# Moving the product of weights and values behind the projection, and the division of the weights to that projection, in the attention of the mixer

## The reference

```python
s = jnp.einsum('bqhd,bqjhd->bhqj', qn[:, :, g], kg).astype(jnp.float32) * scale
s = s + biases[g][:, None, :]
m = jnp.max(s, axis=-1, keepdims=True)
e = jnp.exp(s - m)
l = jnp.sum(e, axis=-1, keepdims=True)
o = jnp.einsum('bhqj,bqjhd->bqhd', e / l, vg.astype(jnp.float32))
...
merged = jax.nn.sigmoid(ga) * (ret @ w_ret_o[l]) + jax.nn.sigmoid(gb) * (att @ w_att_o[l])
x = x + gt_a[:, None, :] * (merged @ w_o[l])
```

## Time and profile before

| | us |
|---|---|
| three runs | 2019.44, 2024.46 and 2028.82; median 2024.46 |
| the profiled execution | 2020.84 |
| its span | 2019.0 |
| PE busy | 1853.7, 92% of the span |
| attention with its fillers, from the trace | about 215 to 339 |
| mean granted clock of PE | 0.968 of full |

### The profile page before, as it was taken

One profiled execution on the slowest core, in us unless ns is written; L12 is line 12 of the kernel. 1 busy time (PEld: TensorE's weight loads), 2 busy tenths in 40 slices (PEclk: granted clock), 3 DMA queues, 4 the chain that ended last, 5 costly groups with the idle time before them and its releaser, 6 DMA issues. The chain is left out here.

```text
span 2019.0 us, 25094 instructions
## 1 busy us (share of the span) xinstructions
PE 1853.7 (92%) x10306; PEld 1214.2 (60%) x10306; DVE 754.2 (37%) x1091; ACT 552.2 (27%) x811; POOL 11.7 (1%) x23
## 2 busy tenths in 40 slices
PE   7999998779999999999999999978899997989998
PEld 6799876643333332333333333328789987869996
DVE  5767644431111111111111111106565555655555
ACT  3444554210000000000000000005544434534442
POOL 0000000000000000000000000000000000000000
PEclk9999999779999999999999999989999998989999
DMA  9877642299999999999999999968345546325552
GB/s 332 311 258 237 235 138 74 96 372 429 431 431 432 431 431 432 431 432 431 431 431 431 431 431 431 431 261 285 125 146 177 180 146 208 117 92 167 188 172 100
DMA packets 152474, 592.99 MB, mean 294 GB/s; under 512 B 7603, under 2 KB 82527, under 8 KB 127824
## 3 DMA queue, kind: packets, MB, share of 16 engines
q1 hardware_dynamic: 150176, 583.90, 73.1%
q0 software_dynamic: 2224, 8.04, 1.2%
HBM read 590.84 MB, written 1.07 MB: 293 GB/s over the span
## 5 line engine op out<-in xcount | busy, mean ns | idle before, releaser
L1426 PE MATMUL psum<-expert_ring,expert_arena 128*64 128x512 f32 x2048 | 453.9, 597 | 21.3 <-DMA expert_ring<-in_w_mlp_dram 21.3
L1426 PEld LDWEIGHTS psum<-expert_ring,expert_arena 128*64 128x64 f32 x2048 | 142.2, 137 | 316.8 <-issue 272.6
L320 DVE TENSOR_TENSOR layer_w_lo<-layer_ring,layer_w_hi 128x1024 fp32r<-128x1024 f32 x190 | 231.4, 1224 | 242.3 <-ACT layer_w_hi L315 242.1
L315 ACT CAST layer_w_hi<-layer_ring 128x1024 fp32r<-128x1024 f32 x190 | 197.6, 1047 | 243.6 <-PE psum L365 123.5
L363 PE MATMUL psum<-layer_x_hi,layer_w_hi 128*128 128x256 f32 x864 | 249.9, 289 | 13.2 <-DVE layer_w_lo L320 10.2
L1442 PE MATMUL psum<-expert_ring,expert_arena 128*64 128x512 f32 x1024 | 234.0, 601 | 30.1 <-DMA expert_ring<-in_w_mlp_dram 29.2
L364 PE MATMUL psum<-layer_x_lo,layer_w_hi 128*128 128x256 f32 x864 | 248.7, 288 | 0.0
L365 PE MATMUL psum<-layer_x_hi,layer_w_lo 128*128 128x256 f32 x864 | 248.5, 288 | 0.0
L1314 DVE TENSOR_SCALAR expert_arena<-psum 128x512 f32<-128x512 f32 x32 | 22.1, 692 | 557.0 <-PE psum L1426 557.0
L363 PEld LDWEIGHTS psum<-layer_x_hi,layer_w_hi 128*128 128x128 f32 x864 | 170.4, 197 | 15.6 <-issue 11.8
L1442 PEld LDWEIGHTS psum<-expert_ring,expert_arena 128*64 128x64 f32 x1024 | 68.7, 137 | 176.1 <-issue 117.8
(11 more groups left out here) (271 smaller groups left out, 1983.9 us busy)
## 6 DMA issues: line engine op xcount, KB each, us to landing
expert_ring<-in_w_mlp_dram SPq DMA_DIRECT2D x192, 2048.0 KB, 23.3
layer_ring<-in_w_ffn_in_dram SPq DMA_DIRECT2D x44, 1024.0 KB, 5.0
mixer_ring<-in_w_in_dram SPq DMA_DIRECT2D x38, 1024.0 KB, 6.8
mixer_ring<-in_w_ada_dram SPq DMA_DIRECT2D x24, 1024.0 KB, 5.9
layer_ring<-in_w_ffn_out_dram SPq DMA_DIRECT2D x20, 1024.0 KB, 4.9
layer_ring<-in_b_w_in_dram SPq DMA_DIRECT2D x10, 1024.0 KB, 7.3
layer_ring<-in_w_mix_out_dram SPq DMA_DIRECT2D x8, 1024.0 KB, 5.0
layer_ring<-in_a_w_in_dram SPq DMA_DIRECT2D x7, 1024.0 KB, 9.2
```

Of the source, the lines that this page charges most:

```text
L315: self.nc.scalar.copy(hi, raw).then_inc(self.hi_ready, 1)
L320: self.nc.vector.tensor_tensor(lo, raw, hi.bitcast(FP32), ALU.subtract).then_inc(self.lo_ready, 1)
L1426: last = nc.tensor.matmul(U[CAP * h:CAP * h + CAP, N * n:N * n + N], xg[:, k, j, :], ring[:, at:at + N], start=False, stop=k == KC - 1)
```

## The change

It has two parts. First, `ao{u-1}` is added behind the projection of step u and, for u = 7, behind the eight `mod` jobs. Second, the division of units 0 to 5 hangs at the first job of the projection of step u (`divided_at`); the divisions of units 6 and 7, whose steps have no projection, still hang at `ao5` and `ao6`.

```diff
--- before.py
+++ after.py
@@ -525,6 +525,7 @@
     filler += [(f"{what}{half}", by, w, col + N * half)
               for what, by, w, col in (("ro", "act", A["w_ret_o"][0], 0), ("ga", "act", w_in, 7680), ("gb", "act", w_in, 8704)) for half in range(2)]
 
+    divided_at = {}
     for u in range(len(units) + 1):
         if u:
             for n in range(1 + units[u - 1][1]):
@@ -532,18 +533,17 @@
         if u < len(units):
             jobs.add(f"sa{u}", "act")
             jobs.add(f"sb{u}", "act")
-        if u > 1:
-            jobs.add(f"ao{u - 1}", "dve", high=True)
-        if filler:
-
+        if filler and u < len(units):
+
+            divided_at[filler[0][0] + "t0"] = u
             for _ in range(2 if u == 1 else 1):
                 name, by, w, col = filler.pop(0)
                 jobs.pair(name, by, jobs.rows(w, col))
-            if u == 1:
-                jobs.add("ao0", "dve", high=True)
         elif u == len(units) - 1:
             for n in range(8):
                 jobs.add(f"mod{2 + n // 4}.{n % 4}", "act")
+        if u:
+            jobs.add(f"ao{u - 1}", "dve", high=True)
         some_ada()
     assert not filler and not ada_left
     for half in range(2):
@@ -771,10 +771,12 @@
                     dve.wait_ge(xh_ready, job.hi)
                     dst, src = high_places(job, b, xl)
                     nc.vector.tensor_tensor(dst, src, high_places(job, b)[0].bitcast(FP32), ALU.subtract).then_inc(freed_by_dve, 1)
-                    if name[:2] == "ao" and 1 < int(name[2:]) + 1 < len(units):
+                    if name[:2] == "ao" and int(name[2:]) + 1 < len(units) and int(name[2:]) + 1 not in divided_at.values():
                         divide(int(name[2:]) + 1)
                     continue
                 if job.by != "dve":
+                    if name in divided_at:
+                        divide(divided_at[name])
                     if name[:2] == "ga":
                         half, t = int(name[2]), int(name[4])
                         cols = slice(N * half, N * half + N)
@@ -790,8 +792,6 @@
                         step.mark(nc.vector.tensor_reduce(mx2[:, u % 2, 0:1], ba, AX.XY, ALU.max))
                         step(nc.vector.tensor_reduce(mx2[:, u % 2, 1:2], b[:, 0:w], AX.X, ALU.max))
                         nc.vector.tensor_reduce(negmax[:, u % 2:u % 2 + 1], mx2[:, u % 2, :], AX.X, ALU.max, negate=True).then_inc(max_ready, 1)
-                        if u < 2:
-                            divide(u)
                     continue
                 if name.startswith("ada"):
                     dve.wait_ge(full, job.index + 1)
```

## The result

The kernel after takes 2035.24 us (median of 8 runs, 2028.99 to 2039.32), the kernel before 2025.65 (8 runs). The ratio is 1.005, 95% interval 1.0035 to 1.0066: slower by 0.5%, about 10 us. The profiled execution took 2034.53 us with a span of 2032.6.

A forecast was written before the change was run, and what follows sets the result against it. The prediction took PE, busy 1853.7 of 2019.0 us, to bound the kernel. Waits of +8.2 us and clock of +3.9 us made +12.1, so 2032.9 from the profiled run or 2036.6 from the median; it took 2035, range 2026 to 2044.

The forecast's parts named there:

- When the division is ready: Behind a projection, the division lets PE start the transposes at E + 3.5 us, E + 3.6 for t = 1.
- E: The moment at which PE has issued the last product of a projection; 268.56 us for ga0.
- New waits less waits that go: Up to `pT5`: transposes wait 13.1 us more for the division; 4.7 us of waits ahead of `ao2` to `ao4` go.
- `pT5` to `pT6`: Mixer stretch without a projection: 6.8 us in place of 9.1, given as -2.3 us.
- `pT6` to `ao7`: End of the attention, `ao6` now behind the `mod` copies: 11.3 us in place of 9.2, given as +2.1 us.
- The clock: After new PE pauses: three falls to half clock, 4.5 us less 0.6 of before, +3.9; bounds -0.6 to 6.9.
- The sum: Whole kernel: waits +8.2 us and clock +3.9 us make +12.1 us; 2032.9 on the profiled execution, 2035 taken.
- The signs: On PE, transposes wait six or seven times for the division, 13 to 16 us; experts' transfers start later than 388.7 us.
- Waits without falls: In the mixer, waits come but the clock falls no more often than before: +7.6 to +8.2 us, 2031; chance 0.27.
- All pauses fall: Every new PE pause in the mixer is followed by a clock fall: +15.1 us, 2038; chance 0.10.
- The filler does fill: Behind projections, division is done when PE reaches the transposes: -5 to -7 us, 2017 to 2019; chance 0.07.
- The change does nothing here: Waits in the mixer only swap places, time within 3 us of before; chance 0.05.

The follow-up runs named there:

- e8_after_fill: Kernel after with throwaway products added in all its PE pauses; 2024.9 us, ratio 1.0010 to the kernel before.
- e7_before_fill: Kernel before with throwaway products added in its PE pauses; 2013.84 us, ratio 0.9947 to the kernel before.
- e2: Kernel before with only the second part: divisions of units 0 to 5 hang at the projections; 2037.97 us, ratio 1.0072.
- e1: Kernel after with only the first part kept: `ao` behind the projection, every division at its own unit's maxima; 2018.6 us, ratio 0.9976 to before.
- e3_third_split: Kernel after with the division behind the third split under each projection, not the fourth; 2020.87 us, ratio 0.9988 to the kernel before.
- e6_tail_only: Kernel after with `ao6` ahead of the eight `mod` jobs again; 2031.18 us, ratio 1.0032 to the kernel before.
- e9_ao_only_fill: Kernel of e1 with throwaway products added in its remaining PE pauses; 2009.02 us, ratio 0.9934 to the kernel before.

## Why the prediction was right, point by point

- **When the division is ready.** Forecast E + 3.5 us, and 3.6 for t = 1. Measured 3.48 behind av2 (230.50 to 233.98) and 3.49 behind ga0 (275.19 to 278.68); behind ga1 3.62 (292.56 to 296.18).
- **New waits less waits that go,** forecast 13.1 - 4.7 = + 8.4 up to `pT5`: with the clock held up on both sides 8.4 (e8_after_fill against e7_before_fill). Each part is in truth some 0.6 us larger. The waits of a profile are counted from the modelled end of a product; between starts, the five transposes come 13.7 us late in all (12.9 by the waits), and 5.3 us go (4.7 by the waits). The two misses cancel. e2 and e1 show the two parts: without the cover of `ao` the transposes wait 3.3 to 3.5 us each; without the late division the move gains 4.3 us.
- **`pT5` to `pT6`,** forecast 6.8 us: 6.8 in e8_after_fill. Against the kernel before I had called this - 2.3 us; 1.0 of it was the slow `ao5` of that execution, not a wait (8.2 in e7_before_fill for 9.1). The sum had that fall at 0.6 in the clock term.
- **`pT6` to `ao7`,** forecast 11.3 us: 11.3 in e8_after_fill, 12.0 in the kernel after with a fall. + 2.1 is right.
- **The clock,** forecast + 3.9 with three falls behind the new pauses. Up to `ao7` the kernel after has three slow stretches (from about 233.8, 329.4 and 346.4 us). Two lie behind new pauses, at `pT0` and `pT5`; the third is later than I had looked. Those two cost 1.55 us (99.57 - 98.02) and 1.3 us (8.12 - 6.81), near the 1.5 of the forecast. By M the slow clock costs 6.5 us after (172.9 - 166.4) and 3.9 before (161.1 - 157.2), so + 2.6. I had charged the kernel before only 0.6 us of its own, for `ao5`, and left out `ao7` and the stretch behind to1 (355.6 to 366.0 us before, 370.3 to 380.7 after), which both kernels have.
- **The clock in the run times.** There its share of the change does not show. The change costs 0.50% as the kernels stand (0.35 to 0.66) and 0.63% with both filled (1.0010 against 0.9947; my estimate from the two intervals is 0.46 to 0.80). If slow clock were part of the price, filling should have made the difference smaller. The waits alone, + 9.2 us, account for the 9.6 to 10 us that were measured; the + 2.6 holds for one pair of executions, and the + 3.9 of the sum is borne out by no run time.
- **The sum,** + 12.1 against the profiled execution: M says 11.8 (9.2 + 2.6). The median moved by 9.6 us (2025.65 to 2035.24). That it fell on the forecast of 2035 to a microsecond is luck. The 2035 lies between 2032.9 and 2036.6 and so stands for 2022.9 + 12.1, where the runs gave 2025.65 + 9.6: the base was 2.8 us too low and the step 2.5 us too long. Nor do the chances gain by it: 0.54 was for slower by over 10.1 us, and 9.6 us by the medians, 0.50% by the ratio, lies on that line.
- **The signs.** The transposes wait for the division seven times and 18.1 us in all (16.2 up to 345 us, and 1.93 at `pT7`), over the 13 to 16 that I had named: in that count I had left out `pT6`, whose wait grew from 1.63 to 3.28 us, though the forecast for `pT5` to `pT6` has it in. The transfers of the experts start at 403.35 us, 14.6 later.
- **The rivals.** *Waits without falls* fails for the profiled execution, which has two falls behind new pauses. By the run times it cannot be told from the forecast: its step of + 7.6 to + 8.2 is about as far below the 9.6 to 10 us as the forecast's 12.1 is above. *All pauses fall* did not come: behind the waits of `pT2` to `pT4` the kernel after shows none. *The filler does fill* is what e3_third_split makes true by moving the division one split ahead, and it then came with the sign that it was given, at about half the size (0.9988, some 2.4 us faster, where the rival had 5 to 7). *The change does nothing here* is refuted by the interval of the ratio and by M.

What stays open: filling the pauses gained more in the run times (0.53% of before, about 10 us; by the ratios also about 8 us from the kernel after to e8_after_fill) than M shows in the profiled pair (3.9 and 6.5 us). Executions of one kernel differ in their mean granted clock (the runs of before from 0.957 to 0.969), and the profiled execution of before was one of its faster ones (2020.84 against a median of 2023 to 2025), so its M may flatter it. Whether the fill also does something behind the mixer was not tested. From the first transfer of the experts to the end of the span the five filled kernels took 1623.6 to 1627.7 us and the seven others 1625.8 to 1632.7, so a few us may lie there.

## What to carry to other kernels

Work that is to cover a wait must still have something to do when the awaited chain starts: here the chain (split, low part, division, 3.5 us) hung behind a piece that is released only by the last product of its own cover, and one piece earlier nearly the whole cost was gone (e3_third_split); with the division back at the maxima, ahead of all the splits, the rest went too (e1_ao_only). Before a step is hung at a job, look where that job stands in the waiting engine's list, splits and copies ahead of it included. And in a kernel bound by PE, read each short pause twice: for its length, and for what the granted clock does behind it.

## What the runs showed of the hardware that I had not expected

Pauses of PE of 2 to 3.5 us between dense stretches are followed by a half clock at some places and not at others: behind the same 2.0 us ahead of `pT2` the clock stayed at 1.00 in the kernel after and was at 0.50 (1.2 GHz) in e6_tail_only. The Trainium skill ("TensorE: Matmul & The Clock Gate", Part 1) says that one kernel measures different numbers of matmuls at the slow clock from run to run, depending on the phase in which the kernel starts. These two profiles fit that, with code that is the same up to there; each kernel has only one profile, so two executions of one kernel were not compared. Nor did every fall follow a pause: in e9_ao_only_fill the clock fell at 327.1 us with PE busy ahead of it. Once down the clock can stay there for long: in e1_ao_only from 329.1 to 342.8 us, 4.6 us of it into the projection to0, which begins at 338.2. Throwaway products in these pauses left av2 to `pT5` at 89.6 us and made the kernel before 0.53% faster (interval 0.39 to 0.67%), and with the better order 0.66% (0.53 to 0.80%).
